# An even order of expert positions, and weight pieces that bring each partition 8 KB in a row

## What is computed

```python
D_MODEL = 1024; SEQ = 512; N_EXPERTS = 32; TOP_K = 4; D_EXPERT = D_MODEL
# x: (1, 512, 1024); w_gate, w_up, w_down: (1, 32, 1024, 1024), float32
    logits = (t @ w_router + b_router).astype(jnp.float32)
    top_val, top_idx = lax.top_k(logits, TOP_K)
    top_w = jax.nn.softmax(top_val, axis=-1)
...
    def expert_block(args):
        xb, e = args
        g = xb @ w_gate[e] + b_gate[e]
        u = xb @ w_up[e] + b_up[e]
        g = jnp.minimum(g, SWIGLU_LIMIT)
        u = jnp.clip(u, -SWIGLU_LIMIT, SWIGLU_LIMIT)
        act = g * jax.nn.sigmoid(SWIGLU_ALPHA * g) * (u + 1.0)
        return act @ w_down[e] + b_down[e]
```

## Time and profile before

| what | value |
|---|---|
| median of 3 runs | 1453.48 us (1450.92 to 1461.56) |
| profiled execution | 1453.4 us, of which the span is 1451.6 us |
| PE busy with matmuls | 1320.3 us, 91% of the span |
| DVE, ACT, POOL busy | 31%, 15%, 13% |
| DMA | 446.16 MB, mean 307 GB/s |
| granted TensorE clock, mean | 0.954 |

### The profile page before, as it was taken

How to read it: one execution, slowest core, us unless ns; L and a number is a source line. 1 busy time by engine, 2 the same in 40 slices (tenths; PEclk the granted TensorE clock), 3 DMA queues, 4 the chain that set the end, 5 groups by cost and what they waited for, 6 DMA issues and landing times.

```text
span 1451.6 us, 40133 instructions
## 1 busy us (share of the span) xinstructions
PE 1320.3 (91%) x18029; PEld 787.9 (54%) x18029; DVE 443.3 (31%) x1030; ACT 217.6 (15%) x491; POOL 192.5 (13%) x148
## 2 busy tenths in 40 slices
PE   5999989996799999899999999999999997876763
PEld 3466676664456656565666666666655554443321
DVE  3653576553322223122132312222222232112110
ACT  2222244341101110101010111111110110100000
POOL 0001300000102211211112121211111211111000
PEclk9999999997799999899999999999999999999765
DMA  8000420019899999999999999999999999999993
GB/s 344 3 1 0 163 88 1 30 49 347 310 352 376 382 391 401 391 393 360 389 387 392 381 381 391 363 385 383 386 386 388 392 380 398 398 395 393 402 406 136
DMA packets 128494, 446.16 MB, mean 307 GB/s; under 512 B 13218, under 2 KB 21474, under 8 KB 128322
## 3 DMA queue, kind: packets, MB, share of 16 engines
q1 hardware_dynamic: 113202, 426.37, 75.5%
q0 software_dynamic: 15120, 17.20, 5.6%
HBM read 433.29 MB, written 14.94 MB: 309 GB/s over the span
## 4 chain that ended last, share of the span: by engine, by line
PE 71%; SPq 19%; DMA 3%; DVE 2%; issue 2%; POOL 1%; ACT 1%; DVEq 0%; POOLq 0%; ACTq 0%
PE pair L1789 46%; SPq L596 18%; PE pair L1548 8%; PE pair L1532 4%; PE pair L1509 2%; PE pair L1640 2%; DMA ring<-in_w_down 1%; PE pair L1749 1%; PE pair L1729 1%; DMA ring<-in_w_in 1%; PE pair L1761 1%; PE pair L1652 1%; DVE rest L1032 1%; POOL ring L699 1%; DMA out<-rest 1%
## 5 line engine op out<-in xcount | busy, mean ns | idle before, releaser
L1789 PE MATMUL pair<-ring,rest 128*32 128x256 f32 x14864 | 864.0, 387 | 52.2 <-DMA ring<-in_w_down 20.1
L1789 PEld LDWEIGHTS pair<-ring,rest 128*32 128x32 f32 x14864 | 473.3, 111 | 391.4 <-issue 46.4
L1032 DVE TENSOR_TENSOR rest<-pair,rest 128x512 f32<-128x512 f32 (+5 forms) x122 | 90.6, 743 | 515.2 <-PE pair L1789 465.5
L751 POOL DMA_INDIRECT out<-rest x82 | 128.5, 1567 | 826.4 <-ACT rest L989 753.6
L1548 PE MATMUL pair<-ring 128*128 128x512 f32 (+1 forms) x320 | 125.3, 550 | 0.0
L989 ACT ACTIVATE rest<-rest 128x256 f32<-128x256 f32 x82 | 36.5, 500 | 568.1 <-DVE rest L1032 568.1
L1548 PEld LDWEIGHTS pair<-ring 128*128 128x128 f32 x320 | 60.3, 190 | 60.4 <-issue 58.8
L1032 DVE TENSOR_TENSOR rest<-rest 128x512 f32<-128x512 f32 (+7 forms) x98 | 62.4, 649 | 34.3 <-ACT rest L971 26.7
L971 ACT ACTIVATE rest<-rest 128x512 f32<-128x512 f32 (+3 forms) x34 | 24.4, 718 | 298.1 <-DVE rest L1341 298.1
L1789 PE MATMUL pair<-rest 128*32 128x256 f32 x880 | 55.7, 395 | 5.7 <-DMA rest<-in_w_gate 3.0
L1532 PE MATMUL pair<-ring 128*128 128x512 f32 x128 | 55.4, 594 | 0.0
(11 more groups left out here) (171 smaller groups left out, 807.0 us busy)
## 6 DMA issues: line engine op xcount, KB each, us to landing
ring<-in_w_up SPq DMA_DIRECT2D x121, 1024.0 KB, 17.3
ring<-in_w_gate SPq DMA_DIRECT2D x120, 1024.0 KB, 15.4
ring<-in_w_down SPq DMA_DIRECT2D x120, 1024.0 KB, 17.9
rest<-in_w_gate SPq DMA_DIRECT2D x8, 1024.0 KB, 17.4
rest<-in_w_down SPq DMA_DIRECT2D x8, 1024.0 KB, 15.9
rest<-in_w_up SPq DMA_DIRECT2D x7, 1024.0 KB, 16.1
ring<-in_w_in SPq DMA_DIRECT2D x1, 4160.0 KB, 15.5
ring<-in_x SPq DMA_DIRECT2D x8, 512.0 KB, 5.9
```

Source lines behind the costliest of these rows:

```text
L751: p.indirect_dma_start(out=out_rows, out_offset=bass.IndirectOffsetOnAxis(ap=sidx[vi.ring][:, g:g + 1].bitcast(I32), axis=0), in_=yrow[:, ...
L1032: return v.tensor_tensor(out=out, in0=a, in1=b, op=op)
L1789: last = T.matmul(ps[q * TOK:(q + 1) * TOK, g * QW:(g + 1) * QW], x, pieces[slot][:, kk, q * QW:(q + 1) * QW], start=(k == 0 and g % 2 == ...
```

## The change

Two things change together.

The order of positions: instead of alternating heavy and light ones under a bound of three groups per position, the rule takes at each position the largest rank left that keeps the running sum of groups within 2.65 groups per position plus 0.5. The groups by position become 3 3 2 3 2 3 3 2 3 3 2 3 2 3 2 2 4 2 2 4 2 2 4 2 2 2 5 2 1 5 1 1. Ranks, their capacities and the 82 groups stay.

The layout of a piece: partition p now holds rows r*256 + 2p and r*256 + 2p + 1, which are 8 KB in a row in HBM. The transposes pick every second column of 256 in place of 128 consecutive ones, so that both operands of a product use the same rows. Sizes, counts and the number of matmuls stay.

```diff
+PACE = 2.65
+
+
 def positions():
 
-    big = [r for r in range(FIXED, NE) if RANK_GROUPS[r] > 2]
-    small = [r for r in range(FIXED, NE) if RANK_GROUPS[r] <= 2]
-    order, work = list(range(FIXED)), sum(RANK_GROUPS[:FIXED])
-    while big or small:
-        if big and (not small or work + RANK_GROUPS[big[0]] <= 3 * len(order) + 2):
-            order.append(big.pop(0))
-        else:
-            order.append(small.pop(0))
-        work += RANK_GROUPS[order[-1]]
+    rest, order, work = list(range(FIXED, NE)), list(range(FIXED)), sum(RANK_GROUPS[:FIXED])
+    while rest:
+        budget = PACE * (len(order) + 1) + 0.5
+        rank = next((r for r in rest if work + RANK_GROUPS[r] <= budget), rest[-1])
+        rest.remove(rank)
+        order.append(rank)
+        work += RANK_GROUPS[rank]
     return order
...
         def piece_source(m, e, r):
 
-            return d[WEIGHTS[m]][0, e].rearrange("(k p) n -> p k n", p=P)[:, r * KP:(r + 1) * KP, :]
+            return d[WEIGHTS[m]][0, e].rearrange("(r p k) n -> r p k n", p=P, k=KP)[r]
...
+            def kp_rows(ap, blocks):
+                return ap.rearrange("p (r i k) -> p r i k", r=blocks, k=KP)
+
             def turn_rows(vi):
...
                     for k in range(4):
-                        last = T.transpose(ps[:, k * c:(k + 1) * c], hrow[vi.b][0:c, (4 * h + k) * P:(4 * h + k + 1) * P],
+                        r, kk = divmod(4 * h + k, KP)
+                        last = T.transpose(ps[:, k * c:(k + 1) * c], kp_rows(hrow[vi.b][0:c, :], PIECES)[:, r, :, kk],
                                            ident[0:c, 0:c])
...
-                    for n in range(min(2, vi.G - 2 * h) * 2):
-                        at_ = 2 * h * QW + n * P
-                        last = T.transpose(ps[:, n * P:(n + 1) * P], ub_b[vi.b][:, at_:at_ + P], ident)
+                    rows = kp_rows(ub_b[vi.b][:, 0:vi.G * QW], vi.G)
+                    for n in range(min(2, vi.G - 2 * h) * KP):
+                        g, kk = divmod(n, KP)
+                        last = T.transpose(ps[:, n * P:(n + 1) * P], rows[:, 2 * h + g, :, kk], ident)
```

## The result

The changed kernel takes 1446.12 us (median of 20 runs, 1443.17 to 1455.58), against 1453.51 of the kernel before (20 runs, 1450.92 to 1461.56). The ratio is 0.995, with a 95% interval of 0.9936 to 0.9963. So it is 7 us faster, where I had forecast 23. The profiled execution has a span of 1443.4 us.

A forecast was written before the change was run, and what follows sets the result against it. The prediction took the whole kernel to be bound by the DMA engines, with few holes. From 1453.4 us it took 8 for the order and 15 for the rows, other terms nothing: 1430 us, range 1407 to 1448.

The forecast's parts named there:

- What bounds the kernel: Whole span from about 360 us: bound by the DMA engines with few holes, in the first stage as in the tail.
- my 34.1 us: Time of a 3-group position in the first stage, taken as what both PE and DMA need for it.
- The order, -8 us: New order of positions fills holes of the DMA engines: 8 us, the middle between 1.5 and 14.
- The list of needs: Positions 5 to 31: 890.8 us taken against a DMA need of 877.1 us, so up to 14 us are holes.
- The windows, which said 1.5 us: At 663 to 700 us the DMA share is 1.00 where 1.04 is full, a hole of 1.5 us.
- The rows, -15 us: Weight loads with rows of 8 KB: 15 us saved, the middle between 0 and 30.
- My fit of two packet sizes: Packets at 11 to 19 and 26.5 to 29 us: 1 ns a packet beside its bytes, so at most 1.0% saved.
- The transposes, 0: PE's transposes of every second column: even if doubled, at most 3.5 us a position, hidden by PE's reserve; cost 0.
- the one on positions 26 and 29: 5-group positions near the end: 83 us to position 29's landed additions against 102 us of loads; just fits, cost nothing.
- the signs that I had named for being wrong: Last slices at 400 GB/s or less; PE idle growing on ACT or DVE, not DMA; holes between 1300 and 1430 us.
- The third rival: Position 29 sets the end: its first visit's additions land 10 us later or more, 7 us lost, 1437; chance 0.06.
- the first, 1445: First rival: the rows bring nothing and the order alone works, 1453 - 8 = 1445; chance 0.22.

The follow-up runs named there:

- the light kernel with rows of 4 KB: New order, two rows of 4 KB; of each product only the first group's matmuls are done, the others left out; 1435.56 us, ratio 0.9869 to the kernel before.
- the one with all matmuls: New order and a separate result buffer for the one-group visit of 5-group positions, weight pieces with two rows of 4 KB; 1452.35 us, ratio 0.9991 to the kernel before.
- the second buffer: Changed kernel, plus an own result buffer for a 5-group position's one-group visit, so DVE need not wait for the first visit's additions; 1431.99 us, ratio 0.9862.
- either remedy: Changed kernel with either an own result buffer for the one-group visit of 5-group positions (1431.99 us) or the ranks of positions 14 and 29 exchanged (1433.07 us).

## Why the prediction was right or wrong

**What bounds the kernel: right for the whole, not shown by the reading.** That the order alone gives 3 us, and that the light kernel with rows of 4 KB (1435.56) is only 17 us below the one with all matmuls (1452.35), both say that PE was nearly level with the loads. But the share of 1.04 at 926 to 1029 us did not show that the loads were at their limit there. The layout alone has 1.02 in the same window with 372 GB/s, though the same rows go at 402 to 412 elsewhere, and PE, busy all of the time, sets the pace. PE waited for nothing from 926 to 1132 us in the kernel before either, and its 34.12 us a position are PE's own time: rows of 8 KB with the same transposes leave them at 34.11. So the first stage was PE's by a little, and my 34.1 us was no measure of what the loads need for 3 groups.

**The order, -8 us: too large, and it depends on the other part.** Alone it measured -3 to -4 us, and without the wait at the 5-group positions some -1. The list of needs had taken 1.35 us a group from positions of 1 to 3 groups; it may be that the 4- and 5-group positions need more than that, and that this came out as holes, but no run separates it. The windows, which said 1.5 us, were nearer. With the faster loads PE holds the old order back in its heavy row, and the order wins 9.

**The rows, -15 us: right in kind, a little small.** 19 us in the kernel, 23 us with most matmuls left out. Of the ends 0 and 30 the middle was a fair choice. My fit of two packet sizes gave at most 1.0% of the 943 us of weights; 2.0 to 2.4% came. Why rows of 8 KB are faster stays open: half the packets, neighbouring rows, and more pieces on their way at once (30.29 us from issue to landing against 20.62) come together in every kernel here. The 358 GB/s that the prediction quotes from the Trainium skill (DMA: Bandwidth & Descriptors, "Where 436 GB/s comes from") were far from the 402 and more of these runs.

**The transposes, 0: right for this order.** They slowed (246 to 282 ns), PE's reserve hid it (1431.67 against 1431.99). In an order whose stretch is bound by PE it costs 6 to 9 us, so the cover I named is what carries it.

**The step that failed is the one on positions 26 and 29**: "It just fits; I cost it at nothing, and at 7 us if the additions become much slower." The 83 us from the first product of position 29 to the landing of its additions were nearly right: from 1328 or so to 1415.4 are 87. What was wrong is the other side of the comparison. I counted 39 more pieces from the moment at which PE starts position 29, as if PE then stood waiting for its first piece. But position 26 had 5 groups too, with a stop of its own of 14.9 us, and only 2 + 1 groups between to catch up. SP had issued the first piece of position 29 48 us before PE was at its first block, and when PE began it, 24 pieces were left to be issued, from this one on:

```profile
1328.42 17.55 SPq L597 DMA_DIRECT2D ring<-in_w_up  x4
```

The other 16 had been issued, and with the one in use before them that is all 17 places. So the loads had run ahead by what the ring holds and then had to stop (share 0.36 and 0.22, some 12 us lost in all). Even so the last pieces came in when the additions landed, at 1415 us, and not 19 us later.

What the wait for the additions had held up was then still to be done, with no piece to hide behind: two products of PE, DVE's steps before and between them, and one more wait for an addition. From the landing to the end of the span it took 28.0 us (1415.37 to 1443.4). With the second buffer there are 16.1 us from the last piece to the end (1413.28 to 1429.4). The 14.0 us between the two profiled kernels are thus 2.1 of later landing and 11.9 of work left behind it.

The second half of the failure is the size of the stop. I had seen that the additions' packets would meet packets twice as long, and gave it no cost but in a rival of 0.06. The last addition landed after 13 us and not 9.15, at both places: 12.94 and 13.00, and 13.68 and 14.21 in the old order.

Two of the signs that I had named for being wrong came: PE's idle time at the end is on ACT and DVE and not on DMA, and DMA has holes between 1300 and 1430 us. The third rival named the mechanism and gave 1437, though it wanted additions 10 us later, and 4 were enough. The time came out near the first, 1445, which is a different thing: there the rows were to bring nothing. They brought their 19 us and gave 13 to 14 back. The total of 1446.1 against 1432 to 1433 with either remedy is this loss. That 1432 is within 2 us of the sum that I had made without it is in part luck: the order was put too high and the rows too low, and the two are not worth the same alone and together.

## What to carry to other kernels

Edits that measure little or nothing one by one can be worth 1.4% together: the rows alone 1.0001, the order alone 0.9975, the order and the second buffer with 4 KB rows 0.9991, all three 0.9862. A part alone tells only whether it stands on what bounds the kernel as it is.

A full DMA share does not prove that the loads are at their limit. Compare the GB/s with the best stretch of the same kernel, and look whether PE ever waits.

A heavy unit of work with a stop in it belongs where lighter work behind it can make up for it, before the next such unit; when costing one near the end, count from where the slower engine will really stand, its lag from the last heavy unit included, and not from a level start.

When packets get longer, look at the short ones that share the engines and at who waits for their landing.

## What the runs showed of the hardware

With the same MB, a piece of 1 MiB whose rows are 8 KB a partition loads faster than one of two rows of 4 KB: 402 against 393 GB/s over some 900 us with PE busy two thirds of the time, and 412 in the tail of the old order, with the DMA share full in all cases. The last piece is longer on its way with 8 KB, 30.29 us from issue to landing against 20.62.

The DMA share was 1.02 both at 372 GB/s, where PE set the pace, and at 412.

An indirect accumulating DMA beside rows of 8 KB landed 12.9 to 14.2 us after its issue, beside rows of 4 KB after 9.15 us (7.96 in the kernel with the new order alone, first row). With the loads over it took 3.77 us (changed kernel, second row):

```profile
1311.14 7.96 DMA out<-rest
```

```profile
1423.77 3.77 DMA out<-rest
```

That the two kinds of packets take turns would explain it; no run here separates that.

TensorE's transposes of float32 with every second column as the stationary operand took longer in the load of that operand too, a median of 140 ns before (first row) and 213 after (second):

```profile
L1749 PEld LDWEIGHTS pair<-rest x272: 133/140/232, 374.9 to 1379.2; 64*128 64x128 f32 x60, 96*128 96x128 f32 x36, 128*128 128x128 f32 x20, 32*128 32x128 f32 x20
```

```profile
L1754 PEld LDWEIGHTS pair<-rest x272: 188/213/226, 375.9 to 1376.4; 64*128 64x128 f32 x60, 96*128 96x128 f32 x36, 128*128 128x128 f32 x20, 32*128 32x128 f32 x20
```
